# An attention and expert trunk: inputs laid out by the host, keys and queries projected in turned form, six spreading products moved into the experts

## What is computed

```python
ml = silu(c) @ mod_w[i] + mod_b[i]              # six vectors of 1024 per layer: shift, scale, gate, twice
hl = xl * (1 + sc1) + sh1                       # hc likewise for the context, from c_ctx
# layer 0: differential attention, 8 heads of 2 x 64, rotary on latent queries and keys
q, k, v = split(h @ wqkv)                       # q of the latent tokens, k and v of latent and context
p = softmax(q k / 8)                            # two maps per head over 512 keys
o = (p[0] - lam * p[1]) @ v; o = o * rsqrt(mean(o * o) + eps) * subln * (1 - lam_init)
yl = o @ wo
# layer 1: four centred averaging windows over the tokens, then a small product per group
xl = layer_norm(ALPHA * xl + (1 + g1) * yl, ln_g, ln_b)
t = xl * (1 + sc2) + sh2
# 16 experts in 4 groups, the best group's two best per token
y2 = sum over the two of w_e * ((silu(t @ wg[e]) * (t @ wu[e])) @ wd[e])
xl = layer_norm(ALPHA * xl + (1 + g2) * y2, ln_g, ln_b)
```

## Time and profile before

| | before |
|---|---|
| median of three runs | 1273.21 us |
| profiled execution: its own time / span | 1275.7 / 1273.4 us |
| PE busy | 1145.6 us (90%) |
| DVE busy | 371.5 us (29%) |
| ACT busy | 170.8 us (13%) |
| DMA over the span | 476.18 MB, 374 GB/s on average |
| mean granted TensorE clock | 0.974 |

### The profile page before, as it was taken

How to read it: one execution, slowest core, us unless ns; L and a number is a source line. 1 busy time by engine, 2 the same in 40 slices (tenths; PEclk the granted TensorE clock), 3 DMA queues, 4 the chain that set the end, 5 groups by cost and what they waited for, 6 DMA issues and landing times.

```text
span 1273.4 us, 12436 instructions
## 1 busy us (share of the span) xinstructions
PE 1145.6 (90%) x5317; PEld 506.3 (40%) x5317; DVE 371.5 (29%) x783; ACT 170.8 (13%) x402; POOL 23.0 (2%) x28
## 2 busy tenths in 40 slices
PE   5979989989899999999999987899999999999995
PEld 3434334554543333343333324633433333433331
DVE  1278889864211111111111113411111111111113
ACT  1100122432310000010000002400100000100000
POOL 0011000000000000000000001000000000000000
PEclk9999989979999999999999998999999999999998
DMA  9788877815799999999999999699999999999993
GB/s 329 290 297 297 328 266 264 321 76 198 317 429 428 427 428 428 428 427 427 427 428 428 427 424 422 289 414 429 427 428 428 428 427 427 427 427 428 428 427 162
DMA packets 54941, 476.18 MB, mean 374 GB/s; under 512 B 5034, under 2 KB 6458, under 8 KB 30308
## 3 DMA queue, kind: packets, MB, share of 16 engines
q1 hardware_dynamic: 42608, 432.92, 81.3%
q0 software_dynamic: 10560, 41.94, 9.0%
q10 hardware_dynamic: 1716, 0.49, 0.2%
HBM read 474.29 MB, written 1.05 MB: 373 GB/s over the span
## 4 chain that ended last, share of the span: by engine, by line
PE 72%; DVE 12%; DMA 11%; issue 3%; ACT 2%; SPq 0%; DVEq 0%
PE ps L793 48%; DMA ring<-in_moe_wu 6%; PE ps L785 5%; DMA ring<-in_mod_w 5%; PE ps L801 4%; PE ps L578 3%; PE ps L655 2%; DVE work L1550 2%; DVE ring L1232 2%; DVE extra L1232 2%; DVE work L1554 2%; PE ps L568 1%; DVE modp L1232 1%; PE ps L809 1%; PE ps L480 1%
## 5 line engine op out<-in xcount | busy, mean ns | idle before, releaser
L793 PE MATMUL ps<-ring,tra 128*64 128x512 f32 x2048 | 447.0, 594 | 3.4 <-DMA ring<-in_moe_wu 2.3
L793 PEld LDWEIGHTS ps<-ring,tra 128*64 128x64 f32 x2048 | 145.8, 137 | 299.7 <-issue 292.8
L793 PE MATMUL ps<-ring,work 128*64 128x512 f32 x1024 | 228.7, 598 | 29.2 <-DVE work L1550 29.2
L793 PEld LDWEIGHTS ps<-ring,work 128*64 128x64 f32 x1024 | 83.1, 137 | 154.2 <-issue 117.4
L578 PE MATMUL ps<-ring 128*128 128x512 f32 x256 | 114.1, 601 | 0.0
L1545 DVE TENSOR_TENSOR work<-ps,work 128x512 f32<-128x512 f32 x32 | 22.1, 692 | 283.4 <-ACT work L1116 283.4
L1116 ACT ACTIVATE work<-ps 128x512 f32<-128x512 f32 x32 | 19.1, 597 | 532.5 <-PE ps L793 532.5
L801 PE MATMUL ps<-work,extra 64*128 64x512 f32 x256 | 63.6, 615 | 25.1 <-DVE work L1554 25.1
L1109 ACT ACTIVATE tra<-ps,cols 128x128 f32<-128x128 f32 x128 | 48.2, 456 | 244.0 <-PE ps L785 244.0
L1548 DVE TENSOR_TENSOR work<-work,ps 128x512 f32<-128x512 f32 x32 | 22.0, 686 | 182.5 <-PE ps L793 182.5
L785 PEld LDWEIGHTS ps<-extra,xn 128*128 128x128 f32 x512 | 62.5, 200 | 25.6 <-issue 22.7
(11 more groups left out here) (186 smaller groups left out, 693.2 us busy)
## 6 DMA issues: line engine op xcount, KB each, us to landing
ring<-in_moe_wg SPq DMA_DIRECT2D x64, 2048.0 KB, 25.1
ring<-in_moe_wu SPq DMA_DIRECT2D x64, 2048.0 KB, 24.2
ring<-in_moe_wd SPq DMA_DIRECT2D x64, 2048.0 KB, 24.2
ring<-in_mod_w POOLq DMA_DIRECT2D x20, 2048.0 KB, 9.5
ring<-in_attn_wqkv SPq DMA_DIRECT2D x6, 2048.0 KB, 14.1
ring<-in_mod_w SPq DMA_DIRECT2D x4, 2048.0 KB, 19.8
ring<-in_attn_wo SPq DMA_DIRECT2D x2, 2048.0 KB, 11.2
xn<-in_x SPq DMA_DIRECT2D x1, 1024.0 KB, 8.6
```

Source lines behind the costliest of these rows:

```text
L793: last = mm(ps[SLOTS * h:SLOTS * h + SLOTS, b, :], lhs(k0 + k), w[:, k, h * NB:(h + 1) * NB], start=(k0 + k == 0), stop=(k0 + k == KT - 1) ...
```

## The change

The host lays out inputs: `mod_w`, `wqkv` and `wo` in units whose rows per partition are 16 KB in one piece (before: eight pieces of 2 KB), latent and context tokens already turned, the condition and the first biases as columns. PE no longer turns tokens; it has short runs of products against the identity between the first spreading products. k and q groups exchange operands, so that results have features in the partitions: a k group is now one head's 128 features by 512 tokens, a q group two heads by 256. Features are reordered so that a rotation's partner lies 32 partitions away; ACT copies every group out of PSUM, issues four transfers of 32 partitions that swap partners, and DVE rotates a whole batch of four heads with three instructions (`rope_batch`), twice before step 0 and at steps 5 and 7. In the softmax the first map is no longer divided by its sum (the head norm takes that in), so one pass over the second map goes. The norm's feature scale moves from DVE to ACT's copy of the turned heads; the norm of the first half moves behind step 15. x itself is loaded last of the early loads. Of eleven spreading products five stay in steps 10 to 15 and six follow the down product of experts 1 to 6 of layer 0.

```diff
+JOBS = ("cols_0", "g1_0", "g1_1", "rpart_0", "gt_0", "cols_2", "cols_1", "joint_0", "joint_1", "rpart_1", "gt_1")
+JOB_AT = {10: (0,), 11: (1,), 12: (2,), 13: (3,), 15: (4,)}
+JOB_BANK = (6, 6, 6, 6, 7, 7, 7, 7, 7, 7, 7)
+EARLY_JOBS = 5
+LATE_JOB = {e: EARLY_JOBS + e - 1 for e in range(1, 7)}
...
+def paired(n):
+
+    import numpy as np
+    return np.arange(n).reshape(-1, 2, 2, HD // 4).transpose(0, 2, 1, 3).reshape(-1)
+
+
+def in_units(w):
+
+    return w.reshape(KT, P, -1, NB).transpose(2, 1, 0, 3).reshape(-1, P, KT * NB)
...
+    given["tokens"] = tokens.T.reshape(KT, P, KEYS).transpose(1, 0, 2).reshape(P, KT * KEYS)
+    given["cond"] = np.stack([c[0], c_ctx]).reshape(2, KT, P).transpose(2, 0, 1).reshape(P, 2 * KT)
+    given["hbias"] = given["mod_b"][0, 0:2 * D].reshape(2, 2, 4, P).transpose(3, 0, 1, 2).reshape(P, 16)
+    given["mod_w"] = np.stack([in_units(w) for w in given["mod_w"]])
+    w = given["attn_wqkv"][0]
+    order = paired(D)
+    given["attn_wqkv"] = in_units(np.concatenate([w[:, 0:D][:, order], w[:, D:2 * D][:, order], w[:, 2 * D:]], 1))
+    given["attn_wo"] = in_units(given["attn_wo"][0])
...
+                if unit != ("k", 0):
+                    load(slot(s), src, sem(f"early_loaded_{s}"))
+                else:
+                    for part in range(2):
+                        c0, c1 = part * UNIT // 2, (part + 1) * UNIT // 2
+                        load(slot(4)[:, c0:c1], tokens[:, c0:c1], sem(f"tokens_loaded_{part}"))
+                        load(slot(s)[:, c0:c1], src[:, c0:c1], sem("first_half_loaded" if part == 0 else f"early_loaded_{s}"))
...
-                pool.dma_start(slot(s).rearrange("p (k n) -> p k n", k=KT), columns(mod_w[layer], m))\
-                    .then_inc(sem(f"sum_loaded_{n % 2}"), 16)
-
-            pool.wait_ge(sem("job_out"), len(JOBS))
+                pool.dma_start(slot(s), mod_w[layer, m]).then_inc(sem(f"sum_loaded_{n % 2}"), 16)
...
+            pe.wait_ge(sem("consts_loaded"), 16)
+            keep_clock(7, 3)
+            pe.wait_ge(sem("cs_ready"), 2)
+            mod_parts(0)
+            keep_clock(7, 1)
+            mod_columns(0)
+            keep_clock(7, 3)
+            mod_parts(1)
+            keep_clock(7, 1)
+            mod_columns(1)
...
+            def multiply(g, k):
+
+                kind, j, t = GROUPS[g]
+                w, first, end = early_slot((kind, j)), k == 0, k == KT - 1
+                if kind == "k":
+                    return mm(bank(acc_bank(g)), w[:, k, t * P:t * P + P], hT[:, k, :], start=first, stop=end)
+                if kind == "v":
+                    return mm(bank(acc_bank(g)), hT[:, k, t * P:t * P + P], w[:, k, :], start=first, stop=end)
+                for n in range(2):
+                    hd = 2 * t + n
+                    last = mm(bank(acc_bank(g), 0, P, n * TOK, (n + 1) * TOK), w[:, k, hd * P:hd * P + P], hT[:, k, 0:TOK],
+                              start=first and n == 0, stop=end, skip_group_check=True)
+                return last
...
-            def turn(g):
-
-                if g in QK_N:
-                    n = QK_N[g]
-                    out_of_psum(g)
-                    if n:
-                        pe.wait_ge(sem("qkT_copied"), n)
-                    turn_blocks(6, nat[n % 2]).then_inc(sem("qkT_done"), 1)
...
-            for s in range(NS + 3):
+            for s in range(NS + 1):
                 for kind, i in FILL[s]:
                     group(i)
-                    turn(prev)
-                    prev = i
                 if 10 + s in BATCH_AT:
                     row_batch(BATCH_AT[10 + s])
                 if s < NS:
                     scores(s)
-                if 2 <= s < NS + 2:
-                    turn_probs(s - 2)
-                if s >= 3:
-                    values(s - 3)
                 if s == NS:
+                    turn_probs(NS - 2)
+                    values(NS - 3)
+                    turn_probs(NS - 1)
+                    values(NS - 2)
+                    values(NS - 1)
                     turn_heads(0)
                     project(0, 0)
+                elif s < NS:
+                    if s >= 2:
+                        turn_probs(s - 2)
+                    if s >= 3:
+                        values(s - 3)
...
                 pe.wait_ge(sem("h_ready"), q + 1)
+                if layer == 0 and e - 1 in LATE_JOB:
+                    pe.wait_ge(sem("job_out"), LATE_JOB[e - 1] + 1)
                 turn_hidden().then_inc(sem("hT_turned"), 1)
...
                     two_halves(6, h_tile, ring_unit(v + 4 + n), 4 * n).then_inc(sem("unit_used"), 1)
+                if layer == 0 and e in LATE_JOB:
+                    job(LATE_JOB[e])
                 pe.wait_ge(sem("ys_ready"), q + 1)
...
+                b = batch_of(g) % 2
+                group_done(act, g)
+                src = bank(acc_bank(g))
+                if kind == "v":
+                    nc.scalar.copy(vv[:, t, j * NB:(j + 1) * NB], src).then_inc(sem("qkv_out"), 1)
                     return
+                if j == 1 and t == 0:
+                    act.wait_ge(sem("roped"), batch_of(g) - 1)
+                if kind == "q":
+                    nc.scalar.copy(raw[b][:, 2 * t:2 * t + 2, :], src.rearrange(by_head, h=2)).then_inc(sem("qkv_out"), 1)
                 else:
+                    nc.scalar.copy(raw[b][:, t, :], src[:, 0:TOK])
+                    nc.scalar.copy(kT[:, HPJ * j + t, TOK:KEYS], src[:, TOK:KEYS]).then_inc(sem("qkv_out"), 1)
+                if t == (1 if kind == "q" else 3):
+                    act.wait_ge(sem("qkv_out"), g + 1)
+                    for n in range(4):
+                        to, of = 32 * n, 32 * (n ^ 1)
+                        load(swapped[b][to:to + 32], raw[b][of:of + 32], f"swapped_{b}")
...
+            def rope_batch(n):
+
+                j, kind = n // 2, n % 2
+                to = qT[j][:, :, :] if kind else kT[:, HPJ * j:HPJ * j + HPJ, 0:TOK]
+                cos, sin = (ropes[:, i, :].unsqueeze(1).to_broadcast([P, HPJ, TOK]) for i in range(2))
+                dve.wait_ge(sem("qkv_out"), 10 * j + (6 if kind else 4))
+                v_.tensor_tensor(to, raw[kind], cos, ALU.mult)
+                dve.wait_ge(sem(f"swapped_{kind}"), 64 * (j + 1))
+                link(v_.tensor_tensor(swapped[kind], swapped[kind], sin, ALU.mult))
+                v_.tensor_tensor(to, to, swapped[kind], ALU.add).then_inc(sem("roped"), 1)
...
-                    link(v_.reciprocal(rs[:, b, :], sm[:, b, :]))
-                    link(v_.tensor_tensor(rl[:, b:b + 1], rs[:, b, 1:2], lam[:, 5:6], ALU.mult))
-                    link(v_.tensor_scalar(pr[b][:, 1, :], pr[b][:, 1, :], rl[:, b:b + 1], None, ALU.mult))
+                    j, t, h = STEPS[s - 1]
+                    link(v_.reciprocal(rs[:, b, 1:2], sm[:, b, 1:2]))
+                    link(v_.scalar_tensor_tensor(out=rl[:, b:b + 1], in0=rs[:, b, 1:2], scalar=lead[:, t, HPJ * j + h:HPJ * j + h + 1],
+                                                 in1=lam[:, 5:6], op0=ALU.mult, op1=ALU.mult))
                     if s >= 3:
                         dve.wait_ge(sem("aT_done"), s - 2)
-                    v_.scalar_tensor_tensor(out=att[b], in0=pr[b][:, 0, :], scalar=rs[:, b, 0:1], in1=pr[b][:, 1, :],
+                    v_.scalar_tensor_tensor(out=att[b], in0=pr[b][:, 1, :], scalar=rl[:, b:b + 1], in1=pr[b][:, 0, :],
                                             op0=ALU.mult, op1=ALU.add).then_inc(sem("att_ready"), 1)
                 if 10 + s < NSUM:
                     unit_sum(10 + s)
                 if s == 3:
```

More of the change, by code:

```diff
@@ L255, in trunk @@
         lam = small[:, 48:56]
+        lead = small[:, 80:96].rearrange("p (t h) -> p t h", t=TT)
         ors = small[:, 64:80].rearrange("p (t h) -> p t h", t=TT)
-        subln = small9[:, 640:768]
-        crow, csig = work[0:2 * KT, 0:P], work[0:2 * KT, P:2 * P]
+        ccol, csig = small[:, 0:16], small[:, 16:32]
         nT = tra[:, :].rearrange("p (k t) -> p k t", k=KT)
@@ L481, in turn_blocks, with early_slot @@
                 return last
+            def early_slot(unit):
+                return slot(EARLY[unit][0]).rearrange("p (k n) -> p k n", k=KT)
             def early(unit):
@@ L560, in finish @@
                 ins.then_inc(sem("unit_used" if t == (1 if kind == "q" else 3) else "qkv_done"), 1)
[L562 to L566 removed]
+            def multiply(g, k):
[10 more added lines that the diff above has]
+                return last
+            def half_group(g, part):
+                kind, j, _ = GROUPS[g]
+                if kind == "k" and part == 0:
+                    pe.wait_ge(sem("first_half_loaded"), 16)
+                else:
+                    early((kind, j))
+                pe.wait_ge(sem("lat_ready"), 4 * part + 4)
+                if kind == "k":
+                    pe.wait_ge(sem("ctx_ready"), 4 * part + 4)
                 for k in range(4 * part, 4 * part + 4):
[L568 removed]
+                    last = multiply(g, k)
```

(16 more changed lines are left out.)

349 lines of the change are left out of this document (134 added, 215 removed).

## The result

The changed kernel takes 1269.31 us in the median of nine runs, the kernel before 1276.82 in nine runs beside them: a ratio of 0.9944, with an interval of 0.9928 to 0.9959, or 0.56% faster. The forecast was 1246, with a range that ended at 1264. The profiled execution took 1269.37 us with a span of 1267.6, against 1275.7 and 1273.4 before; the terms are compared by spans.

What follows compares the result with a forecast made beforehand. Expert 0's start (336.08 us), set by the attention stage's line of DVE work, plus a nearly fixed 937 us. Terms -13.9 - 7.2 - 4.4 - 5.0 + 0.4 + 2.6 = -27.5 gave 1246 us; range 1229 to 1264.

Steps and rivals of the forecast that it cites:

- Start to first sum: From kernel start to DVE's first weighted sum: first sum at 47 instead of 60.85 us, a gain of 13.9 us.
- step 1: Forecast term for kernel start to first weighted sum: first projection near 24 instead of 30.93, gain 13.9 us.
- Ten sums: Ten weighted sums before softmax step 0: 75.7 us, about 9 of it waiting for loads, a gain of 7.2 us.
- the rival: Rotations before step 0: DVE waits for partition-swap transfers; 1257 us if mild, 1295 if severe; chances 0.19 (shared with loads), 0.04.
- The swap's mild price: First two rotations: small loads taking 11.5 us cost about 7 and 4 us, 1257 us; chance 0.19 shared with loads.
- the first rival: Sums in the attention stage: loads stay the bound, only -12 to -15 us left, 1260 us; chance 0.19 shared with swap.
- Steps 0 to 9: Softmax steps 0 to 9: 8.30 us a step without evacuation, 86.4 us against 90.8, a gain of 4.4 us.
- Steps 9 to 15: Softmax steps 9 to 15: spreading products leave, 28.4 us against 33.4 including 1.5 added, a gain of 5.0 us.
- Step 15 to expert 0: Last softmax step to expert 0: first output product 14.3 us after the last maximum; loss 0.4, ends -2 and +5.
- Experts: Layer 0 experts: late jobs behind the second expert matmul cost 3.7 us less one microsecond, a loss of 2.6 us.
- faster: Whole kernel: faster by over 0.5% than the kernel before, chance 0.92.

## Why the prediction was wrong, by its steps

*Start to first sum: failed.* The forecast costed ACT at nothing: "ACT takes over all evacuations and sixteen small DMA issues; its steps use under 4 of 8.3 us, which hides them". That looked at the steps; the issues that hurt are those of the first 30 us, which step 1 left out of PE's path when it put the first projection near 24. They were already in the kernel before, and in the changed one they cost 9.2 us. They became slower (done by 30.2 instead of 10.0) because the rows in the other queues grew, which step 1 counted only as a gain. The rest of the step came out: with the issues out of the way the first sum comes at 47.15.

*Ten sums: failed, by the rival's mechanism.* The swap's mild price was put at 7 and 4 us with a landing of 11.5; it landed in 19.9, DVE waited 14.6 us at the first rotation and at none of the later ones. The rival was sized by a small load among 2 KB rows, but the change itself makes these rows 16 KB. And the rival had only a wait; in the runs the price is that units come late beside the swap, since later rotations alone moved step 0 by 0.3 us and leaving the swap out by 6.3. With the swap off DMA the term is -1.4, not -7.2; what is left is waiting for units, 14.2 us for the 9 of the forecast and no less than before the change, so the first rival is in it too. The forecast's 7.9 us for a unit came from a load that SP had issued; POOL's took 8.4 with the swap on TensorE early.

*Steps 0 to 9: the mechanism right, the size half.* The step of 8.35 us holds, and so does the stall after the row sum (178.71 to 183.20). DVE waited 2.7 us for units, 2.0 of them ahead of the last rotation; without the swap these waits are gone and the stretch takes 85.05, which is 1.3 better than forecast.

*Steps 9 to 15: right* in mechanism, 1.1 us short; the granted clock was 0.79 from 235 to 268 us, lower than the 0.84 of before, and DVE waited 4.4 us for PE where the forecast had added 1.5. *Step 15 to expert 0: right within its ends*; the first output product starts 15.2 us after the last maximum instead of 14.3.

*Experts: right in sum, not in its parts.* 2.9 for 2.6. The column product cost what was forecast, 2.0 for 2.1 in the runs whose scatter behind it had a granted clock of 1.00; the other 1.6 of expert 2's 3.6 is the scatter at 0.54, which no term had. The smaller jobs cost 0.2 or nothing, 1.0 less than forecast, and 1.3 came back in the last expert for the forecast's 1.1. That PE is not held by the weights held true.

*Missing.* The forecast took everything behind expert 0 as fixed. The 5.6 us stall was a row of before that no step read, and it went for a reason outside the change's meaning. That "faster" came true is therefore luck: the parts that the change is made of add up to about nothing. The chances were not added up right either: those named inside the range make 0.92, so 0.08 and not 0.15 was left outside, where the result fell.

## What to carry to other kernels

Here longer rows sped the bulk loads and slowed the small transfers beside them: when rows grow, price again each small load and each engine that issues one, and put issues that are needed late behind the work that is needed early. A wait on a transfer is worth removing only together with what the transfer takes from the others; leave the transfer out once to see its whole price. A stall on PE without a releaser may move with the program, as one of 5.5 us did here: before a gain of 0.5% is given to an edit, look whether such a stall came or went, and shift the program to test it.

## What was not expected of the hardware

Issuing one 8 KB load, behind two of 32 KB, held ACT for 10.06 us with 16 KB rows in the other queue, and 1.70 with 2 KB rows. Transfers of 0.5 MB from SBUF to SBUF brought the engines from about 430 to 350 GB/s for at least 15 us, though they stayed as busy. Forty more records on PE, in a place where it waited, brought a stall of 5.5 us back some 640 us later.
